# Depthwise taps on column groups of TensorE, with u copied under four shifts

## The reference

```
def _conv_module(h, w_pw1, b_pw1, w_dw, b_dw, ln_g, ln_b, w_pw2, b_pw2):
    u = h @ w_pw1 + b_pw1
    u = u[..., :D_MODEL] * jax.nn.sigmoid(u[..., D_MODEL:])
    u = depthwise_conv(u, w_dw, left_padding=CONV_WIDTH - 1) + b_dw    # 31 taps for each channel
    u = jax.nn.silu(_layer_norm(u, ln_g, ln_b))
    return u @ w_pw2 + b_pw2
```

## Time and profile before

| quantity | value |
|---|---|
| three timed runs | 2065.73 us median (2061.25 to 2066.0) |
| the profiled execution | 2065.82 us |
| its span | 2064.0 us, mean granted TensorE clock 0.994 |
| TensorE busy | 2008.3 us, 97% |
| VectorE busy | 1490.7 us, 72% |
| ScalarE busy | 1044.5 us, 51% |
| Pool busy | 123.0 us, 6% |
| DMA | 344.28 MB, mean 167 GB/s |

### The profile page before, as it was taken

One profiled execution on the slowest core, in us unless ns is written; L12 is line 12 of the kernel. 1 busy time (PEld: TensorE's weight loads), 2 busy tenths in 40 slices (PEclk: granted clock), 3 DMA queues, 4 the chain that ended last, 5 costly groups with the idle time before them and its releaser, 6 DMA issues.

```text
span 2064.0 us, 28806 instructions
## 1 busy us (share of the span) xinstructions
PE 2008.3 (97%) x12322; PEld 1770.3 (86%) x12322; DVE 1490.7 (72%) x1750; ACT 1044.5 (51%) x1243; POOL 123.0 (6%) x118
## 2 busy tenths in 40 slices
PE   7999999999999997899999999999999999999999
PEld 6888888888888896788888888788888888888887
DVE  7775767875876599587567757888757765878763
ACT  5544556554554430565455445675545544556542
POOL 1000201000200012100000000010000000201000
PEclk9999999999999998899999999999999999999999
DMA  6656434655565640266565563346555655435653
GB/s 220 194 177 190 128 123 147 193 186 189 185 191 185 194 144 0 84 204 193 174 203 184 180 204 126 123 145 192 188 189 185 189 183 180 130 116 167 193 181 112
DMA packets 329692, 344.28 MB, mean 167 GB/s; under 512 B 8277, under 2 KB 325214, under 8 KB 329566
## 3 DMA queue, kind: packets, MB, share of 16 engines
q1 hardware_dynamic: 329422, 342.41, 52.3%
q10 hardware_dynamic: 144, 0.05, 0.0%
HBM read 341.38 MB, written 1.05 MB: 166 GB/s over the span
## 4 chain that ended last, share of the span: by engine, by line
PE 85%; DVE 8%; ACT 4%; issue 3%; DMA 0%; DVEq 0%; SPq 0%
PE banks L1323 47%; PE banks L1328 24%; PE banks L1314 3%; PE banks L1316 3%; PE banks L1315 3%; DVE sb_w_low L729 2%; DVE sb_x_square L1205 2%; ACT sb_w_high L436 1%; ACT sb_scores L540 1%; PE banks L1513 1%; DMA sb_raw<-in_ffn_w_up 0%; PE banks L1551 0%; DVE sb_neg_max L987 0%; PE banks L1567 0%; PE banks L1534 0%
## 5 line engine op out<-in xcount | busy, mean ns | idle before, releaser
L729 DVE TENSOR_TENSOR sb_w_low<-sb_raw,sb_w_high 128x2048 fp32r<-128x2048 f32 (+1 forms) x332 | 751.8, 2267 | 225.9 <-ACT sb_w_high L436 225.1
L1323 PE MATMUL banks<-sb_x_both,sb_w_high 128*128 128x512 f32 x2816 | 727.3, 394 | 7.1 <-DVE sb_x_both L773 7.1
L436 ACT ACTIVATE sb_w_high<-sb_raw 128x2048 fp32r<-128x2048 f32 (+1 forms) x332 | 618.5, 1867 | 141.0 <-DMA sb_raw<-in_ffn_w_down 118.2
L1323 PEld LDWEIGHTS banks<-sb_x_both,sb_w_high 128*128 128x128 f32 x2816 | 501.1, 189 | 89.6 <-issue 7.4
L1328 PEld LDWEIGHTS banks<-sb_x_both,sb_w_low 128*128 128x128 f32 x2816 | 398.5, 191 | 36.0
L1328 PE MATMUL banks<-sb_x_both,sb_w_low 128*128 128x256 f32 x2816 | 408.2, 282 | 0.0
L1323 PE MATMUL banks<-sb_h_both,sb_w_high 128*128 128x512 f32 x1408 | 360.1, 395 | 0.0
L1323 PEld LDWEIGHTS banks<-sb_h_both,sb_w_high 128*128 128x128 f32 x1408 | 250.4, 188 | 45.6
L1328 PEld LDWEIGHTS banks<-sb_h_both,sb_w_low 128*128 128x128 f32 x1408 | 190.8, 188 | 17.1
L1328 PE MATMUL banks<-sb_h_both,sb_w_low 128*128 128x256 f32 x1408 | 194.3, 279 | 0.0
L1314 PE MATMUL banks<-sb_x_both,sb_w_high 128*128 128x256 f32 x512 | 148.8, 291 | 0.0
(11 more groups left out here) (205 smaller groups left out, 2102.8 us busy)
## 6 DMA issues: line engine op xcount, KB each, us to landing
sb_raw<-in_ffn_w_gate SPq DMA_DIRECT2D x88, 1024.0 KB, 5.3
sb_raw<-in_ffn_w_up SPq DMA_DIRECT2D x88, 1024.0 KB, 5.3
sb_raw<-in_ffn_w_down SPq DMA_DIRECT2D x64, 1024.0 KB, 5.2
sb_raw<-in_ffn_w_down SPq DMA_DIRECT2D x32, 768.0 KB, 4.8
sb_raw<-in_fox_w_in SPq DMA_DIRECT2D x24, 1024.0 KB, 5.3
sb_raw<-in_conv_w_pw SPq DMA_DIRECT2D x12, 1024.0 KB, 5.6
sb_raw<-in_diff_w_in SPq DMA_DIRECT2D x12, 1024.0 KB, 5.1
sb_raw<-in_fox_w_out SPq DMA_DIRECT2D x8, 1024.0 KB, 5.0
```

Source lines behind the costliest of these rows:

```text
L436: act.activation(slot(w_high, b)[:, 0:width(b)], slot(raw, b)[:, 0:width(b)], ACT.Copy).then_inc(S["high_ready"], 1)
L729: dve.tensor_tensor(slot(w_low, b)[:, 0:width(b)], slot(raw, b)[:, 0:width(b)], slot(w_high, b)[:, 0:width(b)].bitcast(F32), ALU.subtract) ...
L1323: return pe.matmul(pair(bank[at][:, :]), high[:, n * P:(n + 1) * P], m_both, start=first, stop=last, skip_group_check=True)
```

## The change

Every tap of every tile goes to TensorE. Channels are taken in groups of 32. A copy of u, `u_shifted`, holds for tile t and channel group g the 32 channels four times, one below the other, each shifted by one more token, so that its 128 rows are 4 shifts x 32 channels. One matmul of 128 rows and 32 output columns then does four taps for 32 channels; the weight matrix is four stacked 32x32 diagonals. Eight rounds (r) of four taps cover 31 taps and one of weight zero, and the four groups write the four 32-partition quarters of one bank. The copies are 16 DMAs a tile, issued by SyncE among the weight loads. Tap weights are loaded at the start by 31 DMAs, one a tap, in place of two. The banks are four (4 to 7), reused for tiles 4 to 7 once ScalarE has copied tiles 0 to 3. VectorE sums the y tiles 0 to 6, and the mean takes two matmuls in place of eight. The splits of blocks 10 to 12 of the phase (three pw2 or next-FFN blocks) now stand among or ahead of the copies out of the banks.

```diff
+SHIFTS, LANE = 4, P // 4
+ROUNDS = -(-TAPS // SHIFTS)
+WINDOW = SEQ + SHIFTS * (ROUNDS - 1)
+PADDED = WINDOW + SHIFTS - 1
...
@@ small_loads (SyncE)
-                taps = rows_of(A["conv_w_dw"][0])
-                for half in range(2):
-                    sp.dma_start(vec_rows[0:124, 2 + half, :], taps[124 * half:124 * half + 124, :]
-                                  ).then_inc(S["vec_loaded"], 16)
+                for k in range(TAPS):
+                    r, shift = k // SHIFTS, k % SHIFTS
+                    rows = slice(32 * (r % 4), 32 * (r % 4) + 32)
+                    sp.dma_start(vec_rows[rows, 2 + r // 4, LANE * shift:LANE * shift + LANE],
+                                 A["conv_w_dw"][0][k:k + 1, :].rearrange("a (t c) -> (a t) c", c=LANE)
+                                 ).then_inc(S["vec_loaded"], 16)
...
@@ SyncE
+            def shift_copies(t):
+                sp.wait_ge(S["u_ready"], t + 1)
+                for shift in range(SHIFTS):
+                    rows = slice(LANE * shift, LANE * shift + LANE)
+                    for g in range(P // LANE):
+                        sp.dma_start(u_shifted[rows, t, g, :],
+                                     u_pad[LANE * g:LANE * g + LANE, t, shift:shift + WINDOW]
+                                     ).then_inc(shifted_landed[t], 16)
...
+                    for n in range(3 * GROUPS):
+                        load(b + n, block_source(n))
+                        if n >= 6 and n % 2 == 0:
+                            if n == 6:
+                                sp.wait_ge(S["pads_ready"], 2)
+                            shift_copies(n - 6)
+                            shift_copies(n - 5)
+                    shift_copies(KT - 2)
+                    shift_copies(KT - 1)
...
@@ Pool
+            def build_tap_weights(t):
+                if t >= 4:
+                    pool.wait_ge(S["taps_done"], t - 3)
+                shape = [P, ROUNDS, P // LANE, LANE]
+                taps = vec[:, DW_COL:VEC_COLS].rearrange("p (r t g) -> p r t g", r=ROUNDS, t=KT)[:, :, t, :]
+                pool.tensor_tensor(tap_weights[:, t % 4, :, :, :],
+                                   lane_of_row[:, :].unsqueeze(1).unsqueeze(1).broadcast_to(shape),
+                                   taps.unsqueeze(3).broadcast_to(shape), ALU.mult
+                                   ).then_inc(S["tap_weights_ready"], 1)
...
@@ ScalarE, conv
-                split_high(b + 2 * GROUPS + 2)
-                for n, (t, at) in enumerate(PE_BANK.items()):
-                    act.wait_ge(S["diagonals_used"], 2 * n + 2)
-                    act.activation(y_conv[:, t, :], bank[at][:, 0:SEQ], ACT.Identity,
+                for t in range(KT):
+                    if t < 3:
+                        split_high(b + 2 * GROUPS + 2 + t)
+                    act.wait_ge(S["taps_done"], t + 1)
+                    act.activation(y_conv[:, t, :], bank[4 + t % 4][:, 0:SEQ], ACT.Identity,
...
-                for k in range(3, 6):
-                    split_high(e + k)
+                split_high(e + 5)
...
@@ VectorE, conv
-                    if j:
-                        more_taps((0, 1), 6 * j - 2, 1, 3)
...
-                more_taps((0, 1), 19, 4, 3)
-                first_taps((2, 3))
-                more_taps((2, 3), 1, 5, 5)
-                split_low(e + 2)
-
-                dve.wait_ge(S["tile_convolved"], 1)
-                dve.wait_ge(S["tap_done"], count[0])
-                more_taps((2, 3, SHARED), SHARED_TAPS, 1, 5)
+                for k in range(2, 5):
+                    split_low(e + k)
+
+                for t in range(1, KT - 1):
+                    dve.wait_ge(S["tile_convolved"], t + 1)
+                    if t > 1:
+                        dve.wait_ge(S["y_sum_step"], t - 1)
+                    dve.tensor_tensor(y_sum, y_sum if t > 1 else y_conv[:, 0, :], y_conv[:, t, :], ALU.add
+                                      ).then_inc(S["y_sum_step"], 1)
...
@@ TensorE, conv
+                for t in range(KT):
+                    pe.wait_ge(shifted_landed[t], 16 * SHIFTS * (P // LANE))
+                    pe.wait_ge(S["tap_weights_ready"], t + 1)
+                    if t >= 4:
+                        pe.wait_ge(S["tile_convolved"], t - 3)
+                    for r in range(ROUNDS):
+                        for g in range(P // LANE):
+                            ins = pe.matmul(bank[4 + t % 4][LANE * g:LANE * g + LANE, 0:SEQ], tap_weights[:, t % 4, r, g, :],
+                                            u_shifted[:, t, g, SHIFTS * r:SHIFTS * r + SEQ],
+                                            start=r == 0, stop=r == ROUNDS - 1, skip_group_check=True)
+                    ins.then_inc(S["taps_done"], 1)
+
+                pe.wait_ge(S["y_sum_step"], KT - 2)
+                pe.matmul(bank[0][:, 0:SEQ], ones[:, :], y_sum, start=True, stop=False, skip_group_check=True)
+                pe.wait_ge(S["tile_convolved"], KT)
+                pe.matmul(bank[0][:, 0:SEQ], ones[:, :], y_conv[:, KT - 1, :], start=False, stop=True,
+                          skip_group_check=True).then_inc(S["mean_done"], 1)
```

More of the change, by code:

```diff
@@ L313, in _, with block_source @@
                 elif kind == "conv":
[L314 to L318, removed]
+                    def block_source(n):
+                        if n < 2 * GROUPS:
+                            return columns(A["conv_w_pw1"][0], n % 2 * D + 256 * (n // 2))
+                        return rows(A["conv_w_pw2"][0], 256 * (n - 2 * GROUPS))
+                    for n in range(3 * GROUPS):
[7 more added lines that the diff above has]
+                    shift_copies(KT - 1)
                 else:
@@ L416, in _ @@
                     pool.memset(u_pad[:, :, 0:TAPS - 1], 0.0).then_inc(S["pads_ready"], 1)
-                    diagonals(range(2, len(TAP_CHUNKS)))
+                    pool.memset(u_pad[:, :, TAPS - 1 + SEQ:], 0.0).then_inc(S["pads_ready"], 1)
+                    for t in range(4, KT):
+                        build_tap_weights(t)
                 if i + 1 < len(phases) and phases[i + 1] == "conv":
@@ L421, in _ @@
                     pool.wait_ge(S["block_done"], starts[i])
-                    diagonals(range(2))
+                    for t in range(4):
+                        build_tap_weights(t)
         @block.scalar
@@ L832, in before_tables @@
                 at = 0
[L833 removed]
+                for col, width in ((PW1_COL, 48), (DW_COL, P), (DW_COL + P, P), (HEAD_COL, 7)):
                     dve.tensor_copy(vec[:, col:col + width], bank[6][:, at:at + width]).then_inc(S["vec_copied"], 1)
@@ L1187, in conv @@
                 b = starts[i]
[L1188 to L1209, removed]
                 for j in range(GROUPS):
@@ L1264, in conv @@
                                       ).then_inc(S["o_bank_free"], 1)
-                for k in range(3, 6):
-                    split_low(e + k)
+                split_low(e + 5)
             dve.memset(eps[:, :], EPS).then_inc(S["dve_consts"], 1)
@@ L1295, in _ @@
                                 ).then_inc(S["dve_consts"], 1)
+            for c in range(P // LANE):
+                rows = slice(LANE * c, LANE * c + LANE)
+                dve.tensor_copy(lane_of_row[rows, :], ident[rows, rows]).then_inc(S["dve_consts"], 1)
             dve.wait_ge(S["norm_turned"], 1)
@@ L1420, in turn_vectors @@
                 at = 0
-                for n, rows in enumerate((48, 124, 124)):
+                for n, rows in enumerate((48, P, P)):
                     pe.transpose(bank[6][:, at:at + rows], vec_rows[0:rows, n + 1, :], ident[0:rows, 0:rows])
@@ L1734, in conv @@
                     columns_half(bank[j % 4], b + j, 1).then_inc(S["block_done"], 1)
-                pe.wait_ge(S["pads_ready"], 1)
-                for n, (t, k0, taps) in enumerate(TAP_CHUNKS):
-                    last_tap = (SHARED_TAPS if t == SHARED else TAPS) - 1
-                    pe.wait_ge(S["u_ready"], t + 1)
-                    pe.wait_ge(S["diagonals_ready"], n + 1)
-                    for k in range(taps):
-                        at = n % 2 * 2048 + k * P
-                        ins = pe.matmul(bank[PE_BANK[t]][:, 0:SEQ], wide[:, at:at + P],
-                                        u_pad[:, t, k0 + k:k0 + k + SEQ],
-                                        start=k0 + k == 0, stop=k0 + k == last_tap)
-                    ins.then_inc(S["diagonals_used"], 1)
@@ L1748, in conv @@
-                for k, t in enumerate((5, 6, 0, 1, 2, 3, SHARED, 7)):
-                    if t > SHARED:
-                        pe.wait_ge(S["tile_convolved"], t - SHARED + 1)
-                    elif t < 2:
-                        pe.wait_ge(S["tap_done"], 2 * TAPS)
-                    else:
-                        pe.wait_ge(S["tap_done"], DVE_TAPS - SHARED + t)
-                    ins = pe.matmul(bank[7][:, 0:SEQ], ones[:, :], y_conv[:, t, :], start=k == 0, stop=k == KT - 1)
-                ins.then_inc(S["mean_done"], 1)
```

(6 more changed lines are left out.)

58 lines of the change are left out of this document (23 added, 35 removed).

## The result

| | before | after |
|---|---|---|
| median of the timed runs (4 each) | 2063.49 us (2060.26 to 2066.0) | 2087.36 us (2085.98 to 2087.79) |
| the profiled execution | 2065.82 us | 2087.5 us |
| its span, mean granted TensorE clock | 2064.0 us, 0.994 | 2085.7 us, 0.984 |

The account below looks back on a forecast made before the run. The prediction took the convolution to be set by VectorE's taps for the last 15 us, TensorE's 51.6 us just under. Sum: 2065.8 - 27 (convolution) + 4 (start) = 2042.8 us, range 2030 to 2061.

Parts of the forecast that it names:

- Rival C: Shift copies on SyncE's queue cost more than assumed: 2069 us at 0.6 us each, 2095 at 0.8; chance 12%.
- Part 2: TensorE's convolution taps: 512 entries in four column groups, 27.8 or 40 us taken with equal weight.
- its best bound: Convolution taps on TensorE with four column groups side by side: 128 x 217 ns, 27.8 us.
- Rivals A and B: Convolution taps: overlap stops at two groups or 119 ns (2058 to 2063 us, 20%); one group alone (2113, 8%).
- the case of 119 ns behind A: Convolution taps at pw1's steady 119 ns an entry: 61 us, gain 6.7; chance 5 of 20%.
- Part 3: Shift copies on SyncE's queue: 128 DMAs at 0.37 us, 47 us in all; load 12 issued at 777.2.
- The stall in pw1: In pw1, block 7 has two microseconds left, so pw1 stalls from 0.44 us a copy on.
- the named signs of being wrong: In the convolution: a stall in pw1 before 757.5, or a last tap after 813.
- Part 4: Convolution's end: tile 6 waits for load 12's split and tile 2's copy, 6.4 us idle; centring gain taken as 27 us.
- Part 5: Kernel start: 31 tap DMAs ahead of load 2 move it to 24.9; cost 3.0 to 5.7 us, taken 4.
- a case of 8: Kernel start: a cost of 8 us with a clock drop in TensorE's gap on top.
- the case of full rate: Convolution taps with four groups at full rate, 3.5 us a tile: centring at 797, gain 30 us.

Follow-up runs that it names:

- e4: The kernel after, its 31 tap DMAs issued four at a time behind the first FFN's weight loads: 2075.17 us, ratio to before 1.0061.
- e8: The kernel after with two tiles a copy, splits of blocks 10 to 12 after the layer norm, tap loads later, `h_both` aligned: 2022.73 us, ratio to before 0.9798.
- e1: A small kernel of DMA issues alone, leaving out the changed kernel's whole trunk: an SBUF-to-SBUF DMA occupied SyncE for 0.63 to 0.65 us.

## Why the prediction was wrong

2043 us were predicted (2030 to 2061); 2087 came. Rival C, with 12%, was the case, and by the condition that it named: copies at 0.57 us or more make the kernel slower.

**Part 2, the overlap: right, at its best bound (27.8 us for all taps).** The fear was that four groups would not run side by side. They do. Between gaps Pool's weights for the next tiles, which wait for the end of a tile each, start every 3.45 us, in the timeline of Pool after:

```profile
783.40 1.94 POOL L433 TENSOR_TENSOR sb_wide<-sb_lane_of_row,sb_vec 128x1024 f32<-128x1024 f32 x1 [54.55 <-PE banks L1747]
786.85 1.94 POOL L433 TENSOR_TENSOR sb_wide<-sb_lane_of_row,sb_vec 128x1024 f32<-128x1024 f32 x1 [1.51 <-PE banks L1747]
790.31 1.94 POOL L433 TENSOR_TENSOR sb_wide<-sb_lane_of_row,sb_vec 128x1024 f32<-128x1024 f32 x1 [1.52 <-PE banks L1747]
```

That is 54 ns for a weight load and an entry, 216 ns for a step of four groups: the full rate of each group. Rivals A and B are out, and so is the case of 119 ns behind A.

The loads of the taps show that they run beside matmuls of the same rows, in their summary after (ns, min/median/max):

```profile
L1747 PEld LDWEIGHTS banks<-sb_u_shifted,sb_wide x512: 106/110/178, 779.6 to 845.3; 128*32 128x32 f32 x171
```

At 110 ns a load and 54 ns a step, two loads are always under way beside matmuls that use all 128 rows. By the Trainium skill ("TensorE: Matmul & The Clock Gate", The mechanism) a load overlaps only where the row groups differ; the trace disagrees. The same section of the Trainium skill also lets a load go ahead where it targets the background weight buffer, an exception that the prediction left out when it took the rule as speaking against the change. The trace agrees with another page of the Trainium skill, "TensorEngine Tiling (Array Packing)", Key Properties: different tiles load and multiply in parallel.

**Part 3, the price of a copy: the step that failed.** The prediction took 0.37 us an issue, from neighbours that all load from HBM, with 0.33 and 0.47 as bounds, and said for rival C that the copies might differ because both their ends are in SBUF. They cost 0.634 alone and 0.67 in place, so that the 128 copies held SyncE for 85.9 us where 47 were expected, and load 12 went 39 us later than expected on the clock of the kernel before (816.3 for 777.2). With 0.67 the prediction's own arithmetic (0.6 gives 2069, 0.8 gives 2095) gives 2078. No row of before showed an SBUF-to-SBUF DMA, and the bounds of an unseen operation were drawn from seen ones of another kind. The stall in pw1 "from 0.44 us a copy on" came, with 7.38 us (TensorE idle from 764.64 to 772.02); it was one of the named signs of being wrong.

**Part 4, the wait: right in kind.** Load 12 behind the last copy, ScalarE's split in front of tile 2's copy, TensorE idle before tile 6, the lower clock after it: all there, with 15.07 us of idle time before tile 6 where 6.4 were expected. Unforeseen were the two earlier gaps, of 4.60 and 11.91 us: blocks 10 and 11 hold up the copies of tiles 0 and 1 in the same way. The stages behind the centring, for which 0 to 2 us were allowed and 0 taken, gave back 2.9 (from the centring to load 131, 21.1 before and 18.2 after).

**Part 5, the start: mis-sized, 10.3 for 4.** The taps' issue took 0.46 us and not 0.37 (of the rows read, the 0.47 of the other DMAs with short pieces over many rows was the nearer), so load 2 went at 26.92 and not at 24.9; it landed 8.1 us later, the slow landing that the row of before showed and that had been discounted towards 5.3. The gap of 8.16 us then brought the lower clock (0.83 from 31.5 to 62 us, 1.00 before), which had been named as a case of 8 and not taken. e4 shows that all of it goes when the DMAs are moved.

**Not in the prediction: 6.3 us from an address.** A wider `vec` moved `h_both`; no step looked at what the new columns shift.

**The sum.** Rival C's arithmetic at 0.67 gives 2078; the start adds 6.3, the address 6.3, and the stages behind the centring give back 2.9: 2087.7, against 2087.5 in the profiled execution. The way there fits too: at 0.67 rival C's arithmetic issues load 12 at 815.2 and centres at 835.4, and on the clock of the kernel before (12.7 us off) they came at 816.3 and 834.5. A gain of the size forecast exists (30 us at the centring in the case of full rate): e8 is 41.2 us ahead there. But e8 is not the forecast kernel with the cost of issue set right, since it also takes the splits out of the path on which the forecast's sum rested.

## What to carry to other kernels

Price a DMA by its issue on the queue that issues it, and for the direction it moves in; an operation that the trace doesn't show needs a measurement or a range as wide as ignorance, not its neighbours' figure. A queue shared with weight loads turns issue time into late weights: count what stands behind the last small DMA, batch tiles into one DMA, and let no engine split a late block ahead of work that others wait for. After any change of a buffer's size, look at the addresses of what is allocated behind it.

## What the runs showed of the hardware

- An SBUF-to-SBUF DMA takes 0.63 to 0.65 us of SyncE's or ScalarE's queue and 0.50 to 0.53 of Pool's, from 16 KB to 142 KB and 32 to 128 rows; one from HBM takes 0.45 at 4 KB to 128 KB. Loads of 8 rows from HBM in the kernel go every 0.33 us.
- In place some issues of copies take longer. In the six kernels with copies, 28 issues took 1.0 to 1.9 us, and each of them overlaps a 16 KB packet on the instruction queue q8; no copy without such a packet beside it took over 0.96 us, though 29 with one beside them kept to 0.6 to 0.7 as well. This was seen side by side, not tested. Five such issues add 4.8 us to the kernel after, which is the difference between its 0.67 a copy and the 0.634 of e1.
- Four column groups of TensorE at 32 columns run fp32 entries of 256 columns at 54 ns each, over 512 entries without a gap in e8, with a weight load for each.
- Streaming 256 columns from an address 32 bytes off a multiple of 64 makes 1408 entries 3.9 to 6.0 us longer (3 to 4 ns each). The entries of 512 columns on the same buffer grow by 0.6 to 0.9 us in all. Other operands were not tried.
